# Gate and up projections in 512-column steps: two units of the next step split ahead of the silu, the up accumulator read one unit earlier

## What is computed

```
D_FF = 5632
h2 = _rms_norm(x, norm2_g)
x = x + (jax.nn.silu(h2 @ w_gate) * (h2 @ w_up)) @ w_down
```

## Time and profile before

| | us |
|---|---|
| median of 3 runs | 1970.33 (1969.72 to 1971.45) |
| the profiled execution: its own time | 1969.52 |
| the profiled execution: span of the profile | 1967.8 |
| PE busy | 1945.1 (99%) |
| PE weight loads busy | 1620.2 (82%) |
| DVE busy | 1363.2 (69%) |
| ACT busy | 998.8 (51%) |
| granted TensorE clock, mean share of full | 0.999 |

### The profile page before, as it was taken

The page is one execution under the profiler, slowest core; times in us unless marked ns, Lnnn a source line. Parts: engine busy times, 40 slices in busy tenths (PEclk is TensorE's granted clock), DMA queues, the critical chain, the costliest instruction groups (busy, mean ns, idle before and its releaser), DMA issues.

```text
span 1967.8 us, 26364 instructions
## 1 busy us (share of the span) xinstructions
PE 1945.1 (99%) x9568; PEld 1620.2 (82%) x9568; DVE 1363.2 (69%) x1619; ACT 998.8 (51%) x1328; POOL 80.0 (4%) x125
## 2 busy tenths in 40 slices
PE   9999999999999999999999999999999999999998
PEld 7888888887888888888778878887777777888887
DVE  6595655556667664655757986768877787678777
ACT  6365444444564554444655564645444545445453
POOL 4000000001200000000300100000000000000000
PEclk9999999999999999999999999999999999999999
DMA  8674555665755444666555435655555555655654
GB/s 288 199 224 129 165 167 163 195 193 157 254 178 194 145 153 147 195 197 186 164 176 161 141 138 182 189 175 190 195 192 171 191 191 183 209 186 193 219 199 160
DMA packets 204538, 360.75 MB, mean 183 GB/s; under 512 B 13201, under 2 KB 53184, under 8 KB 204176
## 3 DMA queue, kind: packets, MB, share of 16 engines
q1 hardware_dynamic: 199792, 346.15, 54.8%
q0 software_dynamic: 4640, 13.20, 2.4%
HBM read 357.20 MB, written 2.10 MB: 183 GB/s over the span
## 4 chain that ended last, share of the span: by engine, by line
PE 90%; DVE 4%; ACT 2%; issue 2%; DVEq 1%; ACTq 1%; DMA 0%; SPq 0%
PE psum L757 21%; PE psum L759 20%; PE psum L758 20%; PE psum L764 6%; PE psum L766 3%; PE psum L1304 2%; PE psum L1305 2%; PE psum L1306 2%; DVE wl L722 2%; DVE x_mixes L2388 2%; PE psum L1550 1%; PE psum L873 1%; PE psum L1238 1%; PE psum L887 1%; PE psum L862 1%
## 5 line engine op out<-in xcount | busy, mean ns | idle before, releaser
L722 DVE TENSOR_TENSOR wl<-raw,wh 128x1024 fp32r<-128x1024 f32 (+2 forms) x595 | 692.9, 1191 | 354.8 <-ACT wh L714 342.9
L714 ACT ACTIVATE wh<-raw 128x1024 fp32r<-128x1024 f32 (+2 forms) x595 | 600.2, 1031 | 519.0 <-PE psum L759 340.8
L757 PE MATMUL psum<-wh,xs 128*128 128x512 f32 (+2 forms) x1440 | 561.5, 390 | 12.3 <-DVE wl L722 5.0
L759 PE MATMUL psum<-wh,xs 128*128 128x512 f32 (+2 forms) x1440 | 553.0, 384 | 0.0
L758 PE MATMUL psum<-wl,xs 128*128 128x512 f32 (+2 forms) x1440 | 552.8, 384 | 0.0
L757 PEld LDWEIGHTS psum<-wh,xs 128*128 128x128 f32 x1440 | 270.5, 188 | 75.4 <-DVE wl L722 9.2
L759 PEld LDWEIGHTS psum<-wh,xs 128*128 128x128 f32 x1440 | 270.5, 188 | 53.5
L758 PEld LDWEIGHTS psum<-wl,xs 128*128 128x128 f32 x1440 | 270.8, 188 | 50.5
L764 PE MATMUL psum<-xs,wh 128*128 128x512 f32 x512 | 181.4, 398 | 0.0
L766 PE MATMUL psum<-xs,wl 128*128 128x256 f32 x512 | 143.3, 280 | 0.0
L757 PE MATMUL psum<-wh,mh 128*128 128x512 f32 x360 | 141.6, 393 | 0.0
(11 more groups left out here) (485 smaller groups left out, 2234.0 us busy)
## 6 DMA issues: line engine op xcount, KB each, us to landing
raw<-in_w_in_dram SPq DMA_DIRECT2D x263, 512.0 KB, 4.5
raw<-in_w_out_dram SPq DMA_DIRECT2D x96, 512.0 KB, 3.8
raw<-in_w_gate_dram SPq DMA_DIRECT2D x88, 512.0 KB, 3.8
raw<-in_w_up_dram SPq DMA_DIRECT2D x88, 512.0 KB, 4.5
raw<-in_w_down_dram SPq DMA_DIRECT2D x80, 512.0 KB, 4.4
cmp_raw<-in_cmp_w_dram SPq DMA_DIRECT2D x16, 512.0 KB, 4.6
raw<-in_w_small_dram SPq DMA_DIRECT2D x16, 336.0 KB, 3.0
bias<-in_b_in_dram POOLq DMA_DIRECT2D x18, 256.0 KB, 4.2
```

Source lines behind the costliest of these rows:

```text
L714: act.activation(shaped(wh[:, n % SPLIT_SLOTS], unit)[:, 0:k, 0:unit.n], shaped(buffer, unit)[:, 0:k, 0:unit.n], ACT.Copy).then_inc(hi_don ...
L722: dve.tensor_tensor(out=shaped(wl[:, n % SPLIT_SLOTS], unit)[:, 0:k, 0:unit.n], in0=shaped(buffer, unit)[:, 0:k, 0:unit.n], in1=shaped(wh[ ...
L757: pe.matmul(o, ah_[:, kt, tok], hi_w, start=first, stop=False)
L759: ins = pe.matmul(o, al_[:, kt, tok], hi_w, start=False, stop=last)
```

## The change

The code that TensorE and SyncE run is the same, instruction for instruction. On ScalarE and VectorE, in steps 1 to 9:

1. Units 0' and 1' (`AHEAD = 2`) are split in the step before theirs: unit 0' in front of the mid at the gate's end, unit 1' behind it. ScalarE takes the silus last of all.
2. The mid at the gate's end holds nothing on ScalarE any more. The silus wait for VectorE's `dve_mid_done` (which follows a drain behind `gate_sum`) in place of the semaphore `gate_summed`, and signal `gate_ready` when done; `up_of_mixes` waits for that.
3. The mid that reads the up accumulator stands behind unit 2 in both lists, where it stood behind unit 3. In step 10 it stays behind unit 3.

The diff, cut to its core:

```
+AHEAD = 2
 ScalarE:
-            def gate_of_mixes(i):
-                act.wait_ge(s("gate_summed"), i)
+            def gate_of_mixes(pl):
+                act.wait_ge(dve_mid_done, pl.slots + 3)
                 act.wait_ge(s("second3_rstd"), TB)
                 for tb in range(TB):
-                    act.activation(silu[:, tb, :], x_mixes[:, 2 * tb, :], ACT.Silu, scale=x_rstd[:, tb:tb + 1])
+                    ins = act.activation(silu[:, tb, :], x_mixes[:, 2 * tb, :], ACT.Silu, scale=x_rstd[:, tb:tb + 1])
+                ins.then_inc(s("gate_ready"), 1)
             def seven_step(i):
-                for n, unit in enumerate(GATE_UP.units):
+                for n, unit in list(enumerate(GATE_UP.units))[AHEAD:]:
-                    if n == 3:
+                    if n == 2:
                         act_mid(pl, -1, 0, nothing)
...
-                act_mid(pl, 1, GATE_END, lambda: gate_of_mixes(i))
+                step_ahead(i + 1, 0)
+                act_mid(pl, 1, GATE_END, nothing)
+                step_ahead(i + 1, 1)
+                gate_of_mixes(pl)
 VectorE:
             def gate_sum():
                 dve.drain()
-                tt(x_mixes[:, 0:3:2, :], acc[0], x_mixes[:, 0:3:2, :], ALU.add).then_inc(s("gate_summed"), 1)
+                tt(x_mixes[:, 0:3:2, :], acc[0], x_mixes[:, 0:3:2, :], ALU.add)
-            def up_of_mixes():
+            def up_of_mixes(i):
                 tt(x_mixes[:, 3:5, :], acc[1], x_mixes[:, 3:5, :], ALU.add)
                 dve.wait_ge(s("second3_rstd"), TB)
+                dve.wait_ge(s("gate_ready"), i)
...
-                    if n == 3:
-                        dve_mid(pl, -1, 0, up_part if isinstance(i, int) else up_of_mixes)
+                    if n == 2:
+                        dve_mid(pl, -1, 0, up_part if isinstance(i, int) else lambda: up_of_mixes(i - FIRST_SEVEN_STEP))
...
+                step_ahead(i + 1, 0)
                 dve_mid(pl, 1, GATE_END, gate_sum)
+                step_ahead(i + 1, 1)
             ffn_step(0, True)
+            step_ahead(FIRST_SEVEN_STEP, 0)
+            step_ahead(FIRST_SEVEN_STEP, 1)
             seven_step(FIRST_SEVEN_STEP)
```

More of the change, by code:

```diff
@@ L2314, in ffn_step @@
                 for n, unit in enumerate(units):
-                    if not (first and n < SLOT_UNITS):
+                    if n >= (SLOT_UNITS if first else AHEAD):
                         split_high(pl, n, unit)
@@ L2333, in first_mix, with step_ahead @@
                 act.activation(x_mixes[:, 0, :], psum[:, 4, :], ACT.Copy).then_inc(s("first_mix"), 1)
-            def gate_of_mixes(i):
-                act.wait_ge(s("gate_summed"), i)
+            def gate_of_mixes(pl):
+                act.wait_ge(dve_mid_done, pl.slots + 3)
                 act.wait_ge(s("second3_rstd"), TB)
                 for tb in range(TB):
-                    act.activation(silu[:, tb, :], x_mixes[:, 2 * tb, :], ACT.Silu, scale=x_rstd[:, tb:tb + 1])
+                    ins = act.activation(silu[:, tb, :], x_mixes[:, 2 * tb, :], ACT.Silu, scale=x_rstd[:, tb:tb + 1])
+                ins.then_inc(s("gate_ready"), 1)
+            def step_ahead(i, n):
+                split_high(ffn_place(i), n, GATE_UP.units[n])
             def seven_step(i):
                 pl = ffn_place(i)
-                for n, unit in enumerate(GATE_UP.units):
+                for n, unit in list(enumerate(GATE_UP.units))[AHEAD:]:
                     if unit.part is None:
@@ L2987, in up_of_mixes, with step_ahead @@
                                              in1=silu[:, tb, :], op0=ALU.mult, op1=ALU.mult)
+            def step_ahead(i, n):
+                split_low(ffn_place(i), n, GATE_UP.units[n])
             def seven_step(i):
                 pl = ffn_place(i)
-                for n, unit in enumerate(GATE_UP.units):
+                for n, unit in list(enumerate(GATE_UP.units))[AHEAD:]:
                     if unit.part is None:
@@ L3015, in ffn_step @@
                     elif n == 3 and not first:
-                        dve_mid(pl, -1, 0, up_of_mixes)
+                        dve_mid(pl, -1, 0, lambda: up_of_mixes(N_SEVEN_STEPS))
                     elif n == 7:
```

## The result

The changed kernel takes 1956.76 us (median of 4 runs, 1956.36 to 1957.07) against 1970.03 us before: 13.3 us less, a ratio of 0.9932 (95% interval 0.9914 to 0.9949). The 1970.03 us are the median of four runs; the 1970.33 us of the prediction were that of the first three. The prediction was 1958.3 us, range 1956.3 to 1963.5. The profiled executions differ by as much: spans 1954.6 and 1967.8 us.

The account below looks back on a forecast made before the run. TensorE, busy 1945.1 of 1967.8 us, bounds the kernel, so only its waits count: 7.3 us at unit 0' plus 5.2 at unit 2', less 0.5 leftovers, gives 12.0 won and 1958.3 us against the median; range 1956.3 to 1963.5.

Parts of the forecast that it names:

- The price of a wait: TensorE in front of units 0' and 2': each wait costs its idle time plus about 0.28 us, together 12.5 us.
- The leftovers: Gaps remaining at TensorE's seams after the change: 0.5 us taken off for all together, bounds 0 and 2.3 us.
- a loop body loaded anew: Doubt about TensorE's jumps back: code loading could keep some gap at eight seams, at most 6.6 us; trace speaks against it.
- The rival of the bare branch: At the seams both waits go but TensorE pays 0.29 us per jump, eight times: 10.2 us won, 1960.1 us; chance 0.12.
- The margin in front of unit 2': TensorE may go on at 1466.85 and wants unit 2' at 1467.4: 0.55 us, the thinnest margin of all.
- I take the whole 0.58 us of before, though the drain has gone from it: ScalarE between the silus and the upper part 2': a 0.58 us gap for the branch, starting that part at 1461.67.
- unit 2' still waits: Rival: the chain to `up_of_mixes` runs 1.2 us later, the old gap returns: 7.3 us won, 1963.0 us; chance 0.10.
- The mark in front of unit 0': TensorE waits there for the drain behind `gate_sum`: handover 0.16 us, ready at 1459.75, 2.2 us before 1461.97.
- The rival on the other side: Slower: late weights of unit 0' hold `gate_sum`, the silus and `up_of_mixes`; at 9.6 us landing, 1988 us; chance 0.02.
- the prediction's rule: In the slower rival, a delay d costs a seam d - 0.55 us in front of unit 2', against 1.46 us before.
- The load for unit 4': Its transfer goes out when the lower part 0' is done, near 1458, where it went out at 1462.79.

Follow-up runs that it names:

- the late lower part: Changed kernel with the lower part of unit 0' formed four times, 3.9 us of extra VectorE work in front of the gate's sum: 1987.72 us, ratio 1.0090.
- The filled kernels: Changed kernel with the lower part of unit 2' formed twice (1957.22 us) or three times (1967.26 us), adding VectorE work in front of the up read.
- Part 3 alone: Kernel before with only the mid that reads the up accumulator moved behind unit 2 in steps 1 to 9, nothing split ahead: 1964.67 us, ratio 0.9974.
- the order with the gate's sum first: Changed kernel with unit 0' split behind the mid at the gate's end on both engines: 1956.94 us; with the lower part 0' formed four times, 1974.03 us.
- the kernel with the sum in front: Changed kernel with unit 0' split behind the gate's sum and its lower part formed four times (3.9 us extra): 1974.03 us, ratio 1.0021.

## Why the prediction held, by its steps

**The price of a wait.** Idle time plus 0.28 us, summed over 17 waits to 12.5 us: right. The sum took in that the nine waits in front of unit 0' aren't alike: 0.67 us idle from step 1 to 2, 0.54 to 0.57 at the seven seams where the loop jumps back, 0.25 from step 9 to 10. From the start of unit 4 in step 1 to that in step 10 it was 1697.72 - 1296.31 = 401.4 us and is 1684.54 - 1295.74 = 388.8 us: 12.6 us shorter. The remaining 0.6 us of the span's 13.2 us had arisen by step 1, before any of the waits. I put that down to the spread between executions, which the runs of one kernel show as well (1956.36 to 1957.07 us); no run shows it apart.

**The leftovers.** I took off 0.5 us, with 2.3 us as the bound of a bare jump. Nothing is left: the step at the seam is the common one, and no gap is there that a loop body loaded anew would leave. Of the 1.5 us between the forecast and the measured time this is 0.5; 0.6 is the spread just named, 0.3 the change of the median of before from three runs to four, and 0.1 the price of the waits. The rival of the bare branch was about right on its price, 0.29 us, which the late lower part brought to light on TensorE (0.84 against 0.55 us), and wrong in that it would show here. It also had one jump too many: eight seams lead into a step of 20 units, but the first of them enters the loop, and only seven jump back. ScalarE's row from step 1 to 2 before the change says the same; its gap is 0.36 us, at the seven jumps it is 0.58 to 0.61:

```profile
1326.14 3.90 ACT L714 ACTIVATE wh<-raw 128x1024 fp32r<-128x1024 f32 x4 [0.36 <-issue]
```

So the bound was 2.0 us. That TensorE jumps while its queued products run is the plainest reading of the unbroken steps. ScalarE too goes on behind the silus without a gap at all nine seams, and the 0.58 us of before was drain and branch in the open.

The Trainium skill, in "Advanced Engine Details and Errata", section Control Flow Timing, puts a compare-and-branch at about 108 ns. The 0.29 us here are another quantity, the difference between a seam where the loop jumps back and one where it doesn't, and no run times the branch by itself; for a jump in the open the measured 0.29 us decides. That nothing of it shows in the changed kernel agrees with the deep queue that the section Engine Queue Depths gives TensorE, though no run here measures the depth.

**The margin in front of unit 2'.** This term was mis-sized: 0.55 us predicted, 1.53 us measured (1.69 us less 0.16). The step that failed is "I take the whole 0.58 us of before, though the drain has gone from it": the upper part 2' follows the silus with no gap (its row starts 0.09 us before theirs ends), which makes 0.67 of the 0.98 us. The silus came 0.2 us sooner and the up read 0.1 us sooner than I had set, which makes the rest. The filled kernels confirm the measured size: 1.3 us more cost nothing, 2.6 us more cost 1.2 us a step. The step didn't touch the forecast time, which had the wait gone either way. The rival "unit 2' still waits" was therefore weaker than the chance I gave it. And part 3 wasn't what won the wait in front of unit 2' in this kernel: with units 0' and 1' ahead, VectorE is early enough with either place. On its own it wins that wait too. The two gains are 5.0 us and 12.2 us alone, and 13.0 us together.

**The mark in front of unit 0'.** I gave its handover 0.16 us, and the late lower part shows 0.55 us, 0.84 with the jump. The margin of 2.2 us covered the mistake. The lower part 0' of before ended at 1461.39 + 1.23 = 1462.62 and not near 1462.55, since 1.14 us is the distance of the starts; nothing hangs on that.

**The rival on the other side.** Its mechanism is real and its price was too low. A delay of 3.9 us in front of the gate's sum made the kernel 18 us slower than before. By the prediction's rule it would be 3.35 - 1.46 = 1.9 us a seam, 17 us. That these agree is luck: the rule put the loss in front of unit 2', while the trace has it in front of unit 0', with the slow clock in it. What makes the case unlikely is what I named: the weights land in time. Here the upper part 0' did wait 0.32 us for them, so less is in hand there than elsewhere.

**The transfers.** The load for unit 4' goes out as forecast, right behind the lower part 0', and ScalarE's waits of over 2 us for it are gone. Part 3 alone shows that the gain in front of unit 2' doesn't come from this. For the wait in front of unit 0' the trace of before does: its weights had landed by 1455.4 at the latest, and its upper part started at 1460.30 behind the silus.

## What to carry to other kernels

When one engine is busy 99% of the time, list the waits that are left with their true price (the distance between starts, not the idle time of the row) and ask for each what stands in the waited-for engine's list ahead of the work. Here two silus and a branch stood ahead of a weight split that needed neither. Work that is only there for a distant reader goes behind work for the next one, but don't put a new dependence in front of the release of an accumulator: the order with the gate's sum first costs nothing measurable, and with 3.9 us of extra work on the lower part it lost 17 us in place of 31.

A part of a change that pays alone may only be margin beside the others. Measure the margin by adding work until it hurts. The margin worked out ahead was nearly three times too small here, two thirds of it through one gap taken over from a place where a drain stood in front of it.

## What the runs showed that I had not expected

- A jump back of the loop costs TensorE 0.24 to 0.32 us if it waits at its mark there (0.79 to 0.87 us from the end of the gate's sum at seven seams, 0.54 and 0.55 at the two without a jump) and nothing if products are queued. ScalarE: 0.29 us in the open, nothing behind queued silus.
- From the end of VectorE's operation to TensorE's product it is 0.05 us for a lower part (1464.87 to 1464.92), 0.16 us for the drained up read, 0.22 us in front of unit 6, and 0.55 us at the mark in front of unit 0'.
- After 1.8 to 2.1 us of idle time in front of unit 0' the granted clock of TensorE fell to 0.50 (the 1.2 GHz level) for about 3 us at six of nine seams. After 1.5 to 1.6 us (the kernel with the sum in front) it fell at none. About 10 of the 31 us lost there are this; the stalls make up 20.5 us.
